# Feed-forward parts of a two-block transformer: three 256-column products a tile in place of sorted 512 and 256

## The reference

```python
D_FF = 2816
def rmsnorm(x, g):
    y = x * lax.rsqrt(jnp.mean(x * x, axis=-1, keepdims=True) + EPS)
    return y * g
def swiglu(x, w_gate, w_up, w_down):
    return (jax.nn.silu(x @ w_gate) * (x @ w_up)) @ w_down
...
h = h + 0.5 * swiglu(rmsnorm(h, ffn1_norm[l]), ffn1_w_gate[l], ffn1_w_up[l], ffn1_w_down[l])
... mixer ...
h = h + 0.5 * swiglu(rmsnorm(h, ffn2_norm[l]), ffn2_w_gate[l], ffn2_w_up[l], ffn2_w_down[l])
```

## Time and profile before

| | us |
|---|---|
| median of the timed runs | 1483.34 |
| the profiled execution's own time | 1479.02 |
| its span, from the first to the last instruction | 1477.2 |
| PE busy | 1463.4 |
| DVE busy | 1160.0 |
| ACT busy | 793.7 |

### The profile page before, as it was taken

How to read it: one execution, slowest core, us unless ns; L and a number is a source line. 1 busy time by engine, 2 the same in 40 slices (tenths; PEclk the granted TensorE clock), 3 DMA queues, 4 the chain that set the end, 5 groups by cost and what they waited for, 6 DMA issues and landing times.

```text
span 1477.2 us, 23028 instructions
## 1 busy us (share of the span) xinstructions
PE 1463.4 (99%) x9666; PEld 1303.5 (88%) x9666; DVE 1160.0 (79%) x1534; ACT 793.7 (54%) x995; POOL 39.3 (3%) x41
## 2 busy tenths in 40 slices
PE   8999999999999999999999999999999999999999
PEld 7888898888988888888889878799999998989978
DVE  7987777787898865988758677879998899766844
ACT  6444455565454443544436566455545645675653
POOL 0000001210000000000001020000000000000000
PEclk9999999999999999999999999999999999999999
DMA  8655545444455545555554544456555454435531
GB/s 318 207 195 197 177 172 192 152 146 169 166 195 191 196 174 202 190 184 195 185 203 142 190 159 156 150 210 214 187 198 186 154 182 151 143 105 189 179 141 57
DMA packets 38390, 262.18 MB, mean 177 GB/s; under 512 B 4624, under 2 KB 5008, under 8 KB 8464
## 3 DMA queue, kind: packets, MB, share of 16 engines
q1 hardware_dynamic: 38144, 260.72, 50.2%
q10 hardware_dynamic: 144, 0.00, 0.0%
HBM read 259.66 MB, written 1.05 MB: 176 GB/s over the span
## 4 chain that ended last, share of the span: by engine, by line
PE 90%; DVE 7%; ACT 1%; DMA 1%; issue 1%; SPq 0%; ACTq 0%
PE ps L301 20%; PE ps L238 13%; PE ps L240 13%; PE ps L239 13%; PE ps L308 10%; PE ps L797 8%; PE ps L802 4%; DVE w_low L223 3%; PE ps L1543 1%; PE ps L326 1%; DVE scratch L2246 1%; DMA w_raw<-in_weights 1%; ACT w_high L217 1%; PE ps L1534 0%; PE ps L1516 0%
## 5 line engine op out<-in xcount | busy, mean ns | idle before, releaser
L223 DVE TENSOR_TENSOR w_low<-w_raw,w_high 128x2048 fp32r<-128x2048 f32 (+2 forms) x244 | 551.6, 2262 | 150.8 <-ACT w_high L217 149.1
L217 ACT ACTIVATE w_high<-w_raw 128x2048 fp32r<-128x2048 f32 (+2 forms) x244 | 460.2, 1887 | 372.6 <-PE ps L308 167.3
L301 PE MATMUL ps<-x,w_high 128*128 128x512 f32 x1328 | 317.5, 392 | 1.2 <-DVE ffn_gate L288 1.2
L301 PEld LDWEIGHTS ps<-x,w_high 128*128 128x128 f32 x1328 | 243.7, 188 | 48.9 <-DVE ffn_gate L288 1.4
L308 PEld LDWEIGHTS ps<-x,w_low 128*128 128x128 f32 x1328 | 166.1, 188 | 6.6
L308 PE MATMUL ps<-x,w_low 128*128 128x256 f32 x1328 | 168.4, 280 | 0.0
L238 PE MATMUL ps<-w_high,x 128*128 128x512 f32 (+1 forms) x448 | 165.1, 369 | 0.0
L240 PE MATMUL ps<-w_high,x 128*128 128x512 f32 (+1 forms) x448 | 160.5, 358 | 0.0
L239 PE MATMUL ps<-w_low,x 128*128 128x512 f32 (+1 forms) x448 | 160.3, 358 | 0.0
L238 PE MATMUL ps<-x,w_high 128*128 128x256 f32 x456 | 129.5, 284 | 0.8 <-DVE x L364 0.8
L797 PE MATMUL ps<-ffn_hid,w_high 128*128 128x512 f32 x528 | 127.7, 392 | 0.0
(11 more groups left out here) (477 smaller groups left out, 2332.5 us busy)
## 6 DMA issues: line engine op xcount, KB each, us to landing
w_raw<-in_weights SPq DMA_DIRECT2D x231, 1024.0 KB, 4.9
w_raw<-in_weights SPq DMA_DIRECT2D x10, 768.0 KB, 4.2
w_raw<-in_weights SPq DMA_DIRECT2D x5, 512.0 KB, 4.1
even_second_vectors<-in_second SPq DMA_DIRECT2D x1, 1836.0 KB, 7.4
setup_first<-in_first SPq DMA_DIRECT2D x3, 512.0 KB, 5.7
resid<-in_x SPq DMA_DIRECT2D x1, 1024.0 KB, 10.6
out<-resid SPq DMA_DIRECT2D x3, 256.0 KB, 2.2
table<-in_table SPq DMA_DIRECT2D x1, 737.0 KB, 9.9
```

The lines of the kernel that those rows point to most:

```text
L217: act.activation(self.slot(self.wh, n), self.slot(self.raw, n), ACT.Copy).then_inc(self.hi_made, 1)
L223: dve.tensor_tensor(self.slot(self.wl, n), self.slot(self.raw, n), self.slot(self.wh, n).bitcast(F32), ALU.subtract).then_inc(self.lo_made, 1)
L301: pe.matmul(c.bank(bank + i).rearrange("p (a t) -> p a t", a=2), wh[:, k, i * P:(i + 1) * P], c.x[:, :, k, :], start=(k == 0), stop=False, ...
```

## The change

Gate, up and apart down slots use the products in threes (`project` and `exact3`), each with 256 columns, both feature tiles in the two halves of one bank. `wide` and `take_wide` go. In the apart parts gate takes bank 0 and 1 by turns and up 2 and 3; in the last part gate takes 0 and 1 by turns, up has bank 2, and bank 3 is the tables' own. The scaling (and at down the residual's update) reads PSUM directly, and PE waits for it, not for the reduction. A slot waits for `lo_made` at its start. The tables of offsets become one: offset 24 (`THREE`) for all feed-forward slots but the named entries at offset 0 (`ENTRY`), which are the slots with the norm's mean and, in the last part, gate slots 23, 26 and 29; the mixer's `S_CKV` and `S_OUT` become entries as well.

```diff
-WIDE, THREE, LOWS, SQUARE, FULL, GLU = 16, -64, -64, 64, 0, 32
...
+TABLE_STEPS = (7, 8, 9)
+TABLE_SLOTS = [3 * s + 2 for s in TABLE_STEPS]
+THREE, SQUARE, FULL, ENTRY = -64, 64, 0, 32
+MIX_ENTRIES, EVEN_ENTRIES = (S_CKV, S_OUT), (A_GLU,)
+def ffn_at(entries):
+    return [below(ENTRY if n in entries else THREE) for n in range(FF_SLOTS)]
...
+FIRST_AT, APART_AT, LAST_AT = ffn_at((2,)), ffn_at((1,)), ffn_at((1, *TABLE_SLOTS))
+AT = (FIRST_AT + MIX_AT + APART_AT + (APART_AT + MIX_AT + APART_AT) * (DEPTH - 2) + APART_AT + MIX_AT + LAST_AT
+      + EVEN_AT + ODD_AT)
...
+def first_parts(c, pe, n, k):
+    for b, (first, _) in enumerate(FIRST_TILES if n == 0 else ()):
+        if k == first:
+            pe.wait_ge(c.xl_made, b + 1)
+            pe.wait_ge(c.lo_made, b + 1)
+    if n == 1 and k % 4 == 0:
+        pe.wait_ge(c.lo_made, PIECES + 1 + k // 4)
...
 def project(c, pe, bank, n, kt, norm=None, tokens=False, width=FC, x=None, midway=None):
-    pe.wait_ge(c.lo_made, c.made(n))
+    if n > 1:
+        pe.wait_ge(c.lo_made, c.made(n))
     for k in range(kt):
+        if n <= 1:
+            first_parts(c, pe, n, k)
...
 class Ffn: vector
-            take_wide(c, dve, b.gate[:, :, :], B_GATE).then_inc(b.gate_read, 1)
...
-            dve.wait_ge(*self.gate_read(s + 1))
-            dve.tensor_tensor(b.gate[:, :, :], b.gate[:, :, :], scale, ALU.mult).then_inc(b.gate_scaled, 1)
+            dve.tensor_tensor(b.gate[:, :, :], c.halves(B_GATE + s % 2), scale, ALU.mult).then_inc(b.gate_scaled, 1)
...
-            take_wide(c, dve, b.up[:, :, :], B_UP).then_inc(b.up_read, 1)
...
+            dve.tensor_tensor(b.up[:, :, :], c.halves(B_UP), scale, ALU.mult).then_inc(b.up_scaled, 1)
...
 class Ffn: tensor
-            if s:
-                pe.wait_ge(*self.gate_read(s))
-            wide(c, pe, B_GATE, base + gate_at(s), norm=None if s else self.norm).then_inc(c.done, 1)
+            if s > 1:
+                pe.wait_ge(*self.gate_scaled(s - 1))
+            project(c, pe, B_GATE + s % 2, base + gate_at(s), DT, norm=None if s else self.norm).then_inc(c.done, 1)
...
-                pe.wait_ge(*self.up_read(s))
-            self.aside.taken(pe, s)
-            wide(c, pe, B_UP, base + up_at(s), midway=None if s else lambda: self.norm.mean(pe)).then_inc(c.done, 1)
+                pe.wait_ge(*self.up_scaled(s))
+            project(c, pe, B_UP, base + up_at(s), DT, midway=None if s else lambda: self.norm.mean(pe)).then_inc(c.done, 1)
...
 class FfnApart: vector, down
-                take_wide(c, dve, b.gate[:, :, :], B_DOWN + 2 * (p % 2)).then_inc(b.down_read, 1)
-                dve.wait_ge(*self.down_read(p + 1))
...
-                dve.scalar_tensor_tensor(out=h, in0=b.gate[:, :, :], scalar=0.5, in1=h, op0=ALU.mult,
+                dve.scalar_tensor_tensor(out=h, in0=c.halves(B_DOWN + p % 2), scalar=0.5, in1=h, op0=ALU.mult,
...
 class FfnApart: tensor (gate and up as above, up with B_UP + s % 2 and up_scaled(s - 1)), down
-                        pe.matmul(c.bank(bank).rearrange("p (a t) -> p a t", a=2), wh[:, j, f], b.hid[:, :, k, :],
-                                  start=(k == 0), stop=False, skip_group_check=True)
...
-                        mm = pe.matmul(c.bank(bank, SEQ), wl[:, j, f], b.hid[:, 0, k, :], start=False,
-                                       stop=(k == FF_TILES - 1), skip_group_check=True)
+                        f = slice(i * P, (i + 1) * P)
+                        mm = exact3(pe, c.halves(B_DOWN + p % 2)[:, i, :], wh[:, j, f], wl[:, j, f], b.hid[:, 0, k, :],
+                                    b.hid[:, 1, k, :], k == 0 and i == 0, k == FF_TILES - 1)
```

More of the change, by code:

```diff
@@ L519, in __init__ @@
         self.hid_high, self.hid_low = Tally(b.hid_high, FF_STEPS * i), Tally(b.hid_low, FF_STEPS * i)
-        self.filled, self.down_read = Tally(c.done, units), Tally(b.down_read, 4 * i)
+        self.filled = Tally(c.done, units)
     def scalar(self, act):
@@ L733, in vector @@
                 self.norm.reciprocal(dve)
-            dve.wait_ge(*self.gate_read(s + 1))
-            dve.tensor_tensor(b.gate[:, :, :], b.gate[:, :, :], scale, ALU.mult).then_inc(b.gate_scaled, 1)
+            dve.tensor_tensor(b.gate[:, :, :], c.halves(B_GATE + s % 2), scale, ALU.mult).then_inc(b.gate_scaled, 1)
             if s:
                 c.split_low(dve, base + 2 * s + RING)
[L738 to L741, removed]
+            dve.wait_ge(*self.filled(2 * s + 2))
+            if s:
+                dve.wait_ge(*self.hid_low(s))
+            dve.tensor_tensor(b.up[:, :, :], c.halves(B_UP + s % 2), scale, ALU.mult).then_inc(b.up_scaled, 1)
             dve.wait_ge(*self.silu_made(s + 1))
@@ L772, in tensor @@
         for s in range(FF_STEPS):
-            if s:
-                pe.wait_ge(*self.gate_read(s))
             mean = lambda: self.norm.mean(pe)
-            wide(c, pe, B_GATE, base + 2 * s, norm=None if s else self.norm,
-                 midway=mean if s == 1 and base == 0 else None).then_inc(c.done, 1)
-            if s:
-                pe.wait_ge(*self.up_read(s))
-            wide(c, pe, B_UP, base + 2 * s + 1, midway=mean if s == 0 and base else None).then_inc(c.done, 1)
+            if s > 1:
+                pe.wait_ge(*self.gate_scaled(s - 1))
+            project(c, pe, B_GATE + s % 2, base + 2 * s, DT, norm=None if s else self.norm,
+                    midway=mean if s == 1 and base == 0 else None).then_inc(c.done, 1)
+            if s > 1:
+                pe.wait_ge(*self.up_scaled(s - 1))
+            project(c, pe, B_UP + s % 2, base + 2 * s + 1, DT, midway=mean if s == 0 and base else None).then_inc(c.done, 1)
         for m in range(FF_STEPS):
@@ L790, in tensor @@
                 if p >= 2 and tiles[0][1] == 0:
-                    pe.wait_ge(*self.down_read(p - 1))
+                    pe.wait_ge(*self.next.fed(p - 2))
                 for j, k in tiles:
```

52 lines of the change are left out of this document (11 added, 41 removed).

## The result

The changed kernel takes 1486.95 us (median of 8 runs, 1485.79 to 1489.11), the kernel before beside it 1481.40 (8 runs, 1478.16 to 1483.92). The ratio is 1.0036 [1.0024, 1.0048]: slower by 0.36%, where 1472 was forecast. The profiled execution took 1485.79 us, its span is 1484.0 (before 1477.2). One later run is left out of its median and ratio, an execution of the kernel with the entry behind the mean that took 2078.60 us at a granted clock of 0.65, where all others lie at 0.995 to 1.000.

What follows compares the result with a forecast made beforehand. The prediction took PE's own pace as the bound (90% of the chain of waits). Its terms, -5.1 - 2.7 - 2.65 - 0.8 = -11.3 us, took the 1483.34 us median to 1472 us, range 1467 to 1487.

Steps and rivals of the forecast that it cites:

- The pace of a slot: Changed slots of 48 products of 256 columns take 5.44 us (fast) or 5.65 (slow), against 5.515 before.
- mean price: Rival, all changed slots: 256-column products average the two prices, 116 ns, 5.57 us a slot; 1489 us, chance 0.05.
- nothing to the pace: Rival: other engines set the slot pace, product order doesn't matter; within 1 us of 1483; 0.08 together with two slow parts.
- The step that failed: Stream at offset 24 behind a mean's entry slot taken as fast: -0.075 us a slot, against +0.135 if slow.
- one part slow by chance: Rival: the first part's stall, or another part by chance, leaves one part slow; -11.3 + 6.3, 1478 us, chance 0.14.
- fast in all: Main case: fast rhythm in all feed-forward parts; 1472 us, its own range 1468 to 1476, chance 0.60.
- the entry doesn't restore the fast rhythm: Rival: behind the mean in slots 1 to 2 of a part the stream stays slow; +8.6 us, 1492 us, chance 0.13.
- A fixed price a matmul: Rule against the change: fixed 2.5 ns per matmul, sixteen more a slot, 4.8 us over 121 slots; near 1488 us.
- First part: First feed-forward part: PE's wait before 33.16 shortened by 0.55 us, 29 fast slots gain 2.2; together -2.7 us.
- One apart part: Second and third feed-forward parts: 32 fast slots, one entry slot and the mean, 180.1 us against 182.68; -2.56 each.
- Last part: Last feed-forward part: 22 slots -1.65 us, eight formerly slow down slots -1.7, four entry slots +0.7; sum -2.65.
- Mixers: S_CKV and S_OUT become entries: -0.2 and -0.6 us in layer 2, 0 in layer 1; taken as -0.8.

## Why the prediction was wrong

*The pace of a slot* (5.44 fast, 5.65 slow, nothing between) was right: in parts 2 to 4 every stretch outside the entry slots is at 113.3 or 117.8. The rivals "mean price" and "nothing to the pace" did not happen.

*The step that failed:* "Bounds for what it leaves behind: fast or slow, as above. I take fast, the row that is nearest." The nearest row had no mean in its entry slot, and it ran in another round: inside that slot the steps of the earlier trace rows lie between 115 and 118, without a 113 or a 120, and the changed kernel's same slot goes 116, 117, 117, the round that is left fast wherever it occurs. With the mean before tile 4 the slot goes in the round of four and is left behind its 120. From there the second and third part run slow, and the last one up to its table slot. Against the mean at tile 5 it cost 13.5 us in parts 2 and 3 (4.06 + 4.27 + 2.57 + 2.56) and 3.6 in the last (1.70 + 1.90). The text itself had the caution, that no row shows this case, and gave the rival 0.13. A coin thrown once for three parts with the same layout falls the same way three times; "one part slow by chance" was the wrong picture of the doubt, and "fast in all" at 0.60 too sure.

*The rival that came true* is "the entry doesn't restore the fast rhythm", at 1487 instead of 1492: the last part was cured at the table slot (+1.70 where the rival had 5.9 - 2.65 = +3.25), the median of before was 1481.4 here, and the first part gained more. *A fixed price a matmul,* by which the prediction comes to 1488 as well, is close to the result by chance: with the mean at tile 5 the same number of matmuls takes 1470.3 us.

*First part:* -3.42 for -2.7. PE's wait is gone altogether, not halved. DVE, with less to do, ends its low part of step 0 at 30.60 in place of 31.97, and the scaling follows from PSUM at once; PE's starts at 32.13 and 32.25 have no idle between them. From that slot on the part takes 157.76 us in place of 160.15 (193.31 - 33.16), -2.39 where the rhythm was priced at -2.2. The other -1.03 is the wait of 1.16 gone, less a start that was a little later. The start itself scatters by more than that: in the ten traces of changed kernels, none of which waits there, that slot begins anywhere from 32.05 to 33.99 us.

```profile
29.91 0.69 DVE L703 TENSOR_TENSOR ffn_hid<-ffn_up,ffn_hid 128x512 fp32r<-128x512 f32 x1 [0.70 <-ACT ffn_hid L663]
30.52 0.68 DVE L690 TENSOR_TENSOR ffn_gate<-ps,rstd 128x512 f32<-128x512 f32 x1
```

*One apart part, given the fast rhythm:* 180.1 us predicted, 180.11 and 180.12 measured with the mean at tile 5. *Last part, likewise:* -1.90 for -2.65; slots 23 to 28 were slow behind the table matmuls, which I had taken as fast. *Mixers:* S_OUT in layer 2 gained 0.6, as priced; the 0.2 of S_CKV there did not come, the stream entered and left it slow. Layer 1 lost 0.58, priced at 0: 0.49 of it in the mixer's slots 3 to 6, behind the 512-column matmuls, where the stream is slow. Which way that interruption throws it differs: with the same mixers the run with the entry behind the mean is fast there, and its layer 1 takes 0.05 less than before. *DVE, banks and added waits:* 0, as priced; the run with one bank and PE's idle time show it. *Sum, given the fast rhythm:* -11.3 predicted; measured -10.4 by the spans at a granted clock of 1.000, -9.6 by the stages of the profiled execution up to the last one.

## What to carry over

When a stream of matmuls has two stable rhythms, what interrupts it is part of its cost: look, in start-to-start steps, at the last step before each change of offset and the first behind it, for the very combination that the change makes, and count the products between. Doubt about a mechanism that repeats with the same layout is one throw for all places, not one for each. And a layout that relies on a phase is fragile: six products fewer behind the mean moved this kernel by 1.1%, from 0.36% slower to 0.74% faster than before; the mean before tile 5 (1470.3 us) has the lowest median of the versions run, though the entry behind the mean (1471.7) and one bank (1471.4) can't be told from it.

## What the runs showed of the hardware that was not expected

The same 256-column product costs 113.3 to 120.2 ns a step, by where in its room the stationary operand begins: the prices at 0 to 60 come back at 64 to 124. At 24, 56 and 120 two prices were seen, 113.3 and 117.8, at 88 the 113.3 alone. At offset 24 the stream keeps the price that it has (959 and 983 products in a row were followed) until something else runs in it. The mean in parts without an entry and the table matmuls toggled it each time. Not every interruption does: the mixer's twelve one-column matmuls left a slow stream slow in the changed kernel (117.8 on either side) and a fast one fast with the mixers' mean at tile 5 (113.3). At offset 0 the steps go in one of three rounds: 113, 116, 118, 120 and 116, 117, 117, both 116.7 a product, or 118, 119, 116, which is 117.8. Where the round of four is cut goes with the price behind it, in 80 of 80 exits. Why the chip does so no run here shows. The Trainium skill's page "TensorE: Matmul & The Clock Gate", section "Back-to-back issue gap", gives 262 cycles for 256 columns at the full clock, as the spacing of an isolated matmul; at 2.4 GHz that is an estimate of 109 ns. These streams show four groups of prices for one size, all above it, and here the measurement decides.
